# A tall stack of small matrix products on one core: order of root, weight halves and first products at each norm

## The reference, cut to what matters

```python
def rmsnorm(x, g):
    xf = x.astype(jnp.float32)
    y = xf * lax.rsqrt(jnp.mean(xf * xf, axis=-1, keepdims=True) + EPS)
    return (y * g.astype(jnp.float32)).astype(x.dtype)
...
    for l in range(DEPTH):
        h = h + mixer(rmsnorm(h, mix_norm[l]))
        h = h + memory_cross_attn(rmsnorm(h, xattn_norm[l]), mem_n, ...)
        h = h + peer_ffn(rmsnorm(h, peer_norm[l]), ...)
    h = rmsnorm(h, final_norm)
...
    for layer in range(DEPTH):
        h = h + mix(_rmsnorm(h, attn_norm[layer]))
        h = h + (silu(gate) * up) @ w_down      # gate, up = _rmsnorm(h, ffn_norm) @ w_gate_up
    return _rmsnorm(h, final_norm)
```

## Time and profile before

| | |
|---|---|
| time, median of 3 runs | 3164.44 us (3161.16 to 3165.61) |
| time of the profiled execution | 3162.43 us |
| its span from first to last instruction | 3160.6 us |
| PE busy | 2929.2 us (93%) |
| PE weight loads busy | 2717.1 us |
| DVE busy | 1972.7 us |
| ACT busy | 1467.7 us |
| POOL busy | 341.2 us |
| granted TensorE clock, mean | 0.938 of full |

### The profile page before, as it was taken

One profiled execution on the slowest core, in us unless ns is written; L12 is line 12 of the kernel. 1 busy time (PEld: TensorE's weight loads), 2 busy tenths in 40 slices (PEclk: granted clock), 3 DMA queues, 4 the chain that ended last, 5 costly groups with the idle time before them and its releaser, 6 DMA issues.

```text
span 3160.6 us, 57237 instructions
## 1 busy us (share of the span) xinstructions
PE 2929.2 (93%) x19610; PEld 2717.1 (86%) x19610; DVE 1972.7 (62%) x4205; ACT 1467.7 (46%) x2397; POOL 341.2 (11%) x166
## 2 busy tenths in 40 slices
PE   7889899999999998858899999999997899999998
PEld 6888799999888888748899999988886779987998
DVE  6545933886576665575497888467775655545554
ACT  4444244444455544434444444455554444443443
POOL 0003684000000000000179000000000000000000
PEclk9998899999999999779899999999998869995999
DMA  4434365545766664323355554666664314450454
GB/s 162 143 126 153 131 209 195 177 171 196 238 237 244 239 221 153 98 41 147 120 170 202 181 180 168 226 251 243 240 241 152 132 54 173 162 226 14 159 179 157
DMA packets 141312, 546.14 MB, mean 173 GB/s; under 512 B 16272, under 2 KB 82080, under 8 KB 84608
## 3 DMA queue, kind: packets, MB, share of 16 engines
q1 hardware_dynamic: 63216, 455.38, 39.8%
q10 hardware_dynamic: 73728, 67.14, 6.7%
q0 software_dynamic: 4240, 21.87, 2.3%
HBM read 503.43 MB, written 40.89 MB: 172 GB/s over the span
## 4 chain that ended last, share of the span: by engine, by line
PE 74%; DVE 10%; DMA 6%; ACT 5%; POOL 4%; issue 2%; SPq 0%; ACTq 0%; DVEq 0%
PE bank L664 22%; PE bank L665 21%; PE bank L666 21%; POOL wL L461 4%; PE bank L820 4%; DMA ring<-in_w_stream 3%; ACT wH L451 3%; DVE wL L461 3%; DMA act_parked<-act_out 2%; PE bank L721 2%; PE bank L739 2%; PE bank L730 1%; DVE act_out L1394 1%; PE bank L677 1%; DVE h L1426 1%
## 5 line engine op out<-in xcount | busy, mean ns | idle before, releaser
L461 DVE TENSOR_TENSOR wL<-ring,wH 128x1024 fp32r<-128x1024 f32 x744 | 907.2, 1225 | 782.0 <-ACT wH L451 781.6
L664 PE MATMUL bank<-hnH,wH 128*128 128x256 f32 x3648 | 1064.2, 292 | 64.2 <-DVE hnL L1400 45.4
L665 PE MATMUL bank<-hnL,wH 128*128 128x256 f32 x3648 | 1044.0, 286 | 0.0
L666 PE MATMUL bank<-hnH,wL 128*128 128x256 f32 x3648 | 1043.2, 286 | 0.0
L451 ACT ACTIVATE wH<-ring 128x1024 fp32r<-128x1024 f32 x864 | 905.7, 1054 | 272.1 <-DMA ring<-in_w_stream 126.2
L664 PEld LDWEIGHTS bank<-hnH,wH 128*128 128x128 f32 x3648 | 709.9, 195 | 73.2 <-issue 57.1
L665 PEld LDWEIGHTS bank<-hnL,wH 128*128 128x128 f32 x3648 | 712.8, 195 | 0.1
L666 PEld LDWEIGHTS bank<-hnH,wL 128*128 128x128 f32 x3648 | 711.3, 195 | 0.0
L664 PE MATMUL bank<-wH,wgtH 128*128 128x512 f32 x1024 | 399.2, 390 | 4.5 <-issue 4.5
L666 PE MATMUL bank<-wH,wgtL 128*128 128x512 f32 x1024 | 399.1, 390 | 0.0
L665 PE MATMUL bank<-wL,wgtH 128*128 128x512 f32 x1024 | 398.9, 390 | 0.0
(11 more groups left out here) (337 smaller groups left out, 3632.9 us busy)
## 6 DMA issues: line engine op xcount, KB each, us to landing
ring<-in_w_stream SPq DMA_DIRECT2D x432, 1024.0 KB, 4.9
act_parked<-act_out ACTq DMA_DIRECT2D x256, 128.0 KB, 3.5
act_in<-act_parked ACTq DMA_DIRECT2D x256, 128.0 KB, 2.7
sw_bias<-in_c_swa POOLq DMA_DIRECT2D x1, 4096.0 KB, 13.9
h_parked<-h POOLq DMA_DIRECT2D x2, 1024.0 KB, 6.5
h_back<-h_parked POOLq DMA_DIRECT2D x2, 1024.0 KB, 6.2
relb_rows<-od_rows POOLq DMA_DIRECT2D x1, 2048.0 KB, 45.3
od_relb<-relb_rows POOLq DMA_DIRECT2D x2, 1024.0 KB, 7.6
```

What stands on the lines that cost most here:

```text
L461: eng.tensor_tensor(wL[:, b % NBUF, :], raw(b), wH[:, b % NBUF, :].bitcast(F32), ALU.subtract).then_inc(w_low, 1)
L664: pe.matmul(dst, lh, rh, start=start, stop=False, skip_group_check=True)
L665: pe.matmul(dst, lh, rl, start=False, stop=False, skip_group_check=True)
L666: return pe.matmul(dst, ll, rh, start=False, stop=stop, skip_group_check=True)
```

## The change

Four things are done:

1. **Root first.** For all norms but `mem` and `x0`, ACT's root and DVE's reciprocal no longer call `feed`. The splits come later: on ACT after the high halves of parts 0 and 1, on DVE ahead of multiplying part 3. An extra square root of one element (L1111 of the changed kernel) stands at the start of `squares`, so that the table is loaded there.
2. **Three outputs side by side.** After a norm, PE works on the first three outputs at once: part 0 for all three, then part 1 for all three, and so on (LEAD = 3).
3. **Down product.** The first two of the three blocks of an output are freed once PE is past them (parts 7 and 15), not at the output's end.
4. **After the peer stage.** ACT and DVE split the next three blocks ahead of waiting for the last v product.

```diff
+LEAD = 3
...
-        lin(f"ffn{l}d", 8, "dve", per=3)
+        for m in range(8):
+            g((f"ffn{l}d", m), "dve")
+            for b in range(3):
+                blocks.append(((f"ffn{l}d", m, b), ("ffd", l, m, b) if b < 2 else (f"ffn{l}d", m)))
...
+            if key[0] == "ffd":
+                return NO[(f"ffn{key[1]}d", key[2])] - 0.5
...
+                elif key[0] == "ffd":
+                    eng.wait_ge(ffd_done, 16 * key[1] + 2 * key[2] + key[3] + 1)
...
-                for m in ms:
+                ms = list(ms)
+                lead = ms[0:LEAD] if first is not None else []
+                held = [bank((name, m)) for m in lead]
+                for k in range(nk if lead else 0):
+                    for m, ps in zip(lead, held):
+                        blk = w((name, m, 0))
+                        if m == lead[0]:
+                            first(k)
+                        last = product(ps[0:width, 0:T], both(blk, FULL, slice(k * width, (k + 1) * width)),
+                                       both(src, FULL, k), k == 0, k == nk - 1)
+                        if k == nk - 1:
+                            last.then_inc(group_done, 1)
+                for m in ms[len(lead):]:
...
+                        if nk > DC and k in (7, 15):
+                            last.then_inc(ffd_done, 1)
...
-                ps = take(key)
+                if key[0] == "norm" and key[1] not in ("mem", "x0"):
+                    assert rank[NO[key]] == reads[0] + 1, key
+                    reads[0] += 1
+                    act.wait_ge(group_done, NO[key] + 1)
+                    ps = psum[bank_of[NO[key]]]
+                else:
+                    ps = take(key)
...
+                act.activation(small[:, 81:82], eps, ACT.Sqrt)
...
                         high((memH if name == "mem" else hnH)[:, c, :], sq[:, c, :])
+                        if c == 1:
+                            feed(act, NO[("norm", name)] + 1)
...
-                fed[id(act)][0] = b0 + 2 * N_KEYS
+                for b in range(b0 + 2 * N_KEYS, b0 + 2 * N_KEYS + 3):
+                    split_high(act, b)
+                fed[id(act)][0] = b0 + 2 * N_KEYS + 3
                 act.wait_ge(v_done, (l + 1) * N_KEYS)
...
-                root(("norm", name))
+                n = NO[("norm", name)]
+                if name in ("mem", "x0"):
+                    feed(dve, n)
+                dve.wait_ge(read_by["act"], rank[n])
+                link(dve.reciprocal(root_sb, root_sb))
                 for c in range(DC + 1):
+                    if c == 3:
+                        feed(dve, n + 1)
```

More of the change, by code:

```diff
@@ L425, in build_stacks @@
         eps_set, sink_set = sem("eps_set"), sem("sink_set")
-        out_done = sem("out_done")
+        out_done, ffd_done = sem("out_done"), sem("ffn_down_block_done")
         def freed_by(b):
@@ L692, in lin @@
                         blk = w((name, m, k // 8))
-                        if first is not None and m == ms[0]:
-                            first(k)
                         last = product(ps[0:width, 0:T], both(blk, FULL, slice(k % 8 * width, (k % 8 + 1) * width)),
                                        both(src, FULL, k), k == 0, k == nk - 1)
+                        if nk > DC and k in (7, 15):
+                            last.then_inc(ffd_done, 1)
                     last.then_inc(group_done, 1)
@@ L876, in ffn @@
                 rms(f)
-                for m in range(FC):
-                    for s in range(2):
-                        ps = bank((f + "gu", m, s))
+                pairs = [(m, s) for m in range(FC) for s in range(2)]
+                held = [bank((f + "gu", m, s)) for m, s in pairs[0:LEAD]]
+                for k in range(DC):
+                    for (m, s), ps in zip(pairs, held):
                         blk = w((f + "gu", m, s))
-                        for k in range(DC):
-                            if m == 0 and s == 0:
-                                normed(f, k)
-                            last = product(ps[:, 0:T], both(blk, FULL, slice(k * P, (k + 1) * P)), both(hn, FULL, k),
-                                           k == 0, k == DC - 1)
-                        last.then_inc(group_done, 1)
+                        if (m, s) == (0, 0):
+                            normed(f, k)
+                        last = product(ps[:, 0:T], both(blk, FULL, slice(k * P, (k + 1) * P)), both(hn, FULL, k),
+                                       k == 0, k == DC - 1)
+                        if k == DC - 1:
+                            last.then_inc(group_done, 1)
+                for m, s in pairs[LEAD:]:
+                    ps = bank((f + "gu", m, s))
+                    blk = w((f + "gu", m, s))
+                    for k in range(DC):
+                        last = product(ps[:, 0:T], both(blk, FULL, slice(k * P, (k + 1) * P)), both(hn, FULL, k),
+                                       k == 0, k == DC - 1)
+                    last.then_inc(group_done, 1)
                 pe.wait_ge(ff_low, FC * (l + 1))
@@ L982, in _ @@
             n96 = [3, 4]
-            for m in range(13):
-                lin("mla_in", [m], hn, width=96 if m in n96 else P,
-                    first=(lambda k: normed("mix2", k)) if m == 0 else None)
+            lin("mla_in", range(3), hn, first=lambda k: normed("mix2", k))
+            for m in range(3, 13):
+                lin("mla_in", [m], hn, width=96 if m in n96 else P)
                 if m == 6:
@@ L1593, in peer @@
                         split_low(dve, b0 + N_KEYS + 3 + c)
-                fed[id(dve)][0] = b0 + 2 * N_KEYS
+                for b in range(b0 + 2 * N_KEYS, b0 + 2 * N_KEYS + 3):
+                    split_low(dve, b)
+                fed[id(dve)][0] = b0 + 2 * N_KEYS + 3
                 dve.wait_ge(v_done, (l + 1) * N_KEYS)
```

## The result

| | before | changed |
|---|---|---|
| median (lowest to highest), 5 runs each | 3161.43 us (3159.39 to 3165.61) | 3143.09 us (3130.40 to 3147.50) |
| profiled execution, its span | 3162.43, 3160.6 us | 3130.40, 3128.6 us |
| PE busy | 2929.2 us | 2907.6 us |
| mean granted clock | 0.938 | 0.944 |

The ratio is 0.9932 (0.9906 to 0.9959): 18 us less. The median is 3143.09 us, where 3141 was forecast. The execution that was profiled is the fastest of the five, 12.7 us under their median. So the two traces differ by 32.0 us and the medians by 18.3, and both numbers have to be explained.

The account below looks back on a forecast made before the run. PE's matmul chain (74% of the span) bounds the kernel, winnable through its idle and lower-clock time; 7.0 + 4.3 - 1.9 - 1.7 + 7.0 + 7.5 + 1.0 = 23.2 us gave a 3141 us median, range 3130 to 3153.

Parts of the forecast that it names:

- Root first: At the norms: PE's idle time falls to the 3.88 us floor, plus 0.6 at the last norm; 7.0 us won.
- rival E: Idle time moves to splits inside the parts, PE waits for part 2 instead; 3161 us, no measurable change; 8%.
- Three side by side: First 72 matmuls behind eight norms: gain between 0 (unchanged clock) and 8.6 us (mix1's clock); middle taken, 4.3 us.
- The formula: First 72 matmuls after a norm take 8.6 us plus half the time spent at the lower clock.
- rival C: Copies and splits after three outputs aren't covered; fifth block 1 to 2 us late at eight places; 3151 us; 24%.
- Behind the peer stages: Adds after the v products start sooner, 5.6 us at the first peer stage and 1.9 at the second; 7.5 us.
- Down product: PE's waits at the second block of the next output, and so both 3.5 us stalls, go; 7.0 us won.
- rival D: A table load now on a path holds ACT up for twice its 1.28 us, three places; 3145 us; 4%.
- the first stage: Splits ahead of window sums and extra root before mem's squares, less earlier first outputs; net loss 1.9 us.
- x0: PE needs three splits for part 0 instead of one, 1.5 us, plus 0.2 for the extra root; loss 1.7 us.
- 0.8 us earlier: First stage: root ahead of the first four splits ends the first three outputs 0 to 1.7 us earlier; 0.8 taken.
- clock for norm sums: After the peer stages, PE's shorter idle time may keep the clock up for norm sums; 1.0 us, bounds 0 and 4.

Follow-up runs that it names:

- root_only: Kernel before with only the root moved ahead of the splits, extra root and split inside the parts, outputs one after the other; 3169.26 us, ratio 1.0014.
- trim_keys: The changed kernel with both the edits of trim and that of keys_before; 3114.19 us, ratio 0.9834 to the kernel before.
- keys_before: Kernel before, with PE waiting for the four rotated queries a half of the key products reads, not all eight; 3142.08 us, ratio 0.9929.
- trim: Changed kernel without interleaving at mix0 and x0, extra root dropped before mem's and x0's squares, moved earlier behind peer stages; 3130.93 us, ratio 0.9889.
- down_only: Kernel before with only the down product's first two blocks per output freed at parts 7 and 15; 3157.40 us, ratio 0.9965.
- early_only: Kernel before with only three of four splits put ahead of the wait for the last v product, on ACT and DVE; 3159.74 us, ratio 0.9967.
- lead_only: Kernel before with only the first three outputs side by side (LEAD = 3 and PE's loop); 3156.49 us, ratio 0.9963.
- before_shift: Kernel before with 24 extra overwritten matmuls in each peer stage's sixth query output, starting the key products later; 3163.09 us, ratio 0.9984.
- after_shift: Changed kernel with 7 extra overwritten matmuls in the sixth query output, starting the key products 0.8 us later; 3142.28 us, ratio 0.9931.
- after_again: The changed kernel run once more, unaltered, on the chip of the two shifted kernels; 3138.30 us, ratio 0.9924.
- after_keys: The changed kernel with the edit of keys_before (PE waits for four rotated queries, not eight); 3122.55 us, ratio 0.9855.
- trim_keys_one: trim_keys with LEAD = 1: first outputs one after the other at every norm, root still ahead of the splits; 3127.72 us, ratio 0.9881.

## Why the prediction was right, and where it was not

**Right in size, and for the most part by its mechanism.** *Root first*, 7.0 forecast: the idle times fell to 3.87 at all eight places, 6.5 us, and the last root starts 2.86 us after the last square's start instead of 3.62, 0.8 more; 7.3. root_only adds the condition that the prediction named in rival E: alone, the idle time goes over to part 2, and the median wins nothing. *Three side by side*, 4.3 forecast as the middle between an unchanged clock and mix1's: 3.9 measured, with three short stretches at the lower clock and five long ones, so the size is right. The mechanism is not quite the one foreseen. The formula, 8.6 us and half the time at the lower clock, gives 10.3 for 3.4 us of it and 11.65 for 6.1, and 10.20 and 11.38 were measured: with starts 0.213 us apart instead of 0.120, a microsecond at the lower clock costs 0.44 us and not 0.5. The changed kernel spends 39.8 us of the eight stretches at the lower clock and before 42.2, worth 1.1 us. The other 2.8 us are the pace of the parts, to which the prediction gave nothing where the lower clock lasts 5.5 us: with 5.5 us of it mix2 took 11.38 us before and mix3 takes 11.12 now, and with 3.4 us mix1 took 11.09 before and takes 10.20 now. The half had filled in for it. That both errors nearly cancel is luck. The burst behind the three outputs costs PE nothing in the eight places (rival C). *Behind the peer stages*, 5.6 and 1.9: the first went from 10.44 to 4.79, 5.65, and the second from 6.68 to 4.79 (sums at 2399.76 and adds at 2406.44 before, 2383.81 and 2388.60 now), 1.89. *Down product*, 7.0: 7 times 0.55 in each of the two, 7.7. The load of the table with the extra root costs 1.4 us and no more; the row of 1.28 with the root 0.01 us behind it is against rival D.

One idle time of 3.87 us was followed by stretches of 10.2 us in three places and of 11.1 to 11.4 in five, and which places they were changed from kernel to kernel (peer1 11.35 in the changed kernel, 10.19 in trim_keys). The Trainium skill (TensorE: Matmul & The Clock Gate, What's actually happening) says that the hardware watches activity in windows that run free of the kernel, and that the point of change depends on where the first matmul lands in one. The traces agree with that rule: neither value belongs to a norm, and at the key products too it was the place on the beat that decided.

**Too small: the losses at the start.** The prediction had 1.9 for the first stage and 1.7 for x0. Measured were 3.5 until x0's first product and 4.1 behind it, 7.6 in all. The step that failed is the one at x0: I counted the splits that PE would wait for and not the clock. PE started before all three splits were done, worked in pieces, and its first 72 matmuls ran at 0.74 instead of 1.00 and took 3.16 us more. That is the same term that I had for the eight norms, left out in the one place where before had no lower clock to start with. The lower clock does not hang on the side-by-side outputs alone: all five profiles that have them at x0 show it (11.5 to 12.3 us for the 72), but so does one of the nine without, keys_before, whose program is that of before up to here and which idled the same 2.94 us:

```profile
174.39:185.74 11.35, 11.35 (x73) 0.73 0.64 230
```

In the first stage the term "0.8 us earlier" for the first three outputs did not make up for the rest, and of mem's sum after it the clock was lower too (16 matmuls took 6.73 us, 5.38 before). trim, which takes both back, is 0.9889 against 0.9932.

**Not seen: the key products.** Waits of 1.0 and 1.35 us were too short for me to look at what follows them. They decide over 0 to 18.5 us between two profiles, more than any term of my sum. How much of the scatter is theirs is not shown; root_only's two groups lie 20 us apart with four falls in the profile of the lower one. My reading is that the sum held because the falls still come in most executions of the changed kernel, as far as its median tells (12.7 us over an execution with none is two or three falls of 4.7); they were not counted in those executions. Had they gone for good, as in the profiled one, the result would have been near 3130, at the lower edge of my range, for a reason that was not in it. That the forecast lies 2 us from the median is thus partly luck: losses 4.0 too small, the down products' gain 0.7 too small, and the "clock for norm sums" (1.0) never shown.

What stays open: why before and its three first variants reach all four key products at a moment that brings the fall, how many falls an unprofiled execution has, and what takes the 60 us of lower clock behind mix2 away in root_only's profile.

## What to carry to other kernels

A root or any other short step moved to the head of a queue pushes the work behind it onto the next consumer; it pays only together with something that gives that consumer other work (root_only 1.0014 in the median, interleaving worth 13.5 us with it). Look at the granted clock behind every wait of the matrix engine, also the one-microsecond ones, and above all where narrow matmuls follow: take such a wait away by waiting for what is read, not for the whole batch. And where a cause of clock falls is left in, one profile says little of the median: compare several executions before giving a gain to the edit.

## What the runs showed of the hardware

A wait of 1.00 or 1.35 us ahead of 48 matmuls with 128 columns was followed by 10.2 us at 1.2 GHz (13.7 in a few places), starting 1.1 to 2.6 us after the first of them, in all 16 places of four kernels' profiles (before, root_only, down_only, early_only), and in 6 of the 24 places of six others (lead_only, the changed kernel, before_shift, after_shift, after_again, trim). Without the wait it came in none of 16 (keys_before, after_keys, trim_keys, trim_keys_one), where the 48 matmuls took 5.5 to 5.8 us. A fall of 10.2 us cost 4.4 to 4.7 us, since at the lower clock matmuls of 128 columns start 0.213 us apart, the same as those of 256, and at the full clock 0.111. Whether the fall came hung on where the place lay on the beat of the clock's changes, at all 40 places with the wait, and a shift of a microsecond is enough to change that: so an edit at one end of a program can win or lose up to 18.5 us at the other, in a profile, without touching it.
